# Unread products while the last modulation tile loads, a longer slack for later modulation loads, and a last unit in two halves

## The reference

```python
def adaln(c, w_ada, b_ada):
    mod = jax.nn.silu(c) @ w_ada + b_ada  # (B, 6D)
    return [m[:, None, :] for m in jnp.split(mod, 6, axis=-1)]

sh1, sc1, g1, sh2, sc2, g2 = adaln(c, w_ada[l], b_ada[l])
h = modulate(y_s, norm1_w[l], sh1, sc1)       # rms_norm(x, w) * (1 + scale) + shift
q, k, v, u, g = project_mixers(h, w_in[l], q_norm_w[l], k_norm_w[l])
...
y_s = y_s + g1 * (jnp.concatenate([att, sgu], axis=-1) @ w_o[l])
h = modulate(y_s, norm2_w[l], sh2, sc2)
y_s = y_s + g2 * sq_relu_mlp(h, w_ff1[l], w_ff2[l])
```

## Time and profile before

| | |
|---|---|
| Time, median of 3 runs | 2461.25 us (2461.22 to 2461.75) |
| The profiled execution | 2461.3 us |
| Span of its slowest core (core 7) | 2459.1 us |
| Spans of the other cores | 2451.1 to 2458.5 us |
| TensorE busy, core 7 | 2356.5 us (96%) |
| VectorE, ScalarE, GpSimd busy, core 7 | 1066.5, 721.3, 207.4 us |
| Mean granted clock of TensorE | 0.980 to 0.982 |

### The profile page before, as it was taken

One profiled execution on the slowest core, in us unless ns is written; L12 is line 12 of the kernel. 1 busy time (PEld: TensorE's weight loads), 2 busy tenths in 40 slices (PEclk: granted clock), 3 DMA queues, 4 the chain that ended last, 5 costly groups with the idle time before them and its releaser, 6 DMA issues.

```text
span 2459.1 us, 38418 instructions; the slowest of 8 cores (2451.1 to 2459.1 us)
## 1 busy us (share of the span) xinstructions
PE 2356.5 (96%) x16224; PEld 1351.2 (55%) x16224; DVE 1066.5 (43%) x2129; ACT 721.3 (29%) x1185; POOL 207.4 (8%) x376
## 2 busy tenths in 40 slices
PE   2578999999999999999999999999999999999999
PEld 2367888787888854444444444444444444444444
DVE  2148763754732153553101332322524626528347
ACT  3056675765746561322231001001010010010110
POOL 2101121121100030000110000000000000000000
PEclk7679999999999999999999999999999999999999
DMA  9995786886625186966562222222433423323346
GB/s 208 171 218 156 110 118 94 110 115 111 101 50 83 32 135 140 255 202 129 87 108 52 52 52 52 52 52 52 90 65 64 90 52 75 80 50 81 64 94 188
DMA packets 168728, 251.56 MB, mean 102 GB/s; under 512 B 101104, under 2 KB 106864, under 8 KB 154480
## 3 DMA queue, kind: packets, MB, share of 16 engines
q0 software_dynamic: 54240, 164.94, 39.0%
q1 hardware_dynamic: 114320, 84.17, 13.9%
HBM read 348.28 MB, written 32.67 MB: 155 GB/s over the span
## 4 chain that ended last, share of the span: by engine, by line
PE 92%; DMA 5%; ACT 1%; another core or an unknown queue 1%; DVE 0%; POOL 0%; issue 0%; DVEq 0%; POOLq 0%
PE ps L454 92%; DMA ada<-wa 3%; DMA wr<-wa 1%; DMA xt<-xs 1%; ACT xn L487 0%; PE ps L464 0%; ACT hT L487 0%; POOL ada L575 0%; ACT P L487 0%; DVE xn L516 0%; DVE hT L516 0%; POOL wr L575 0%; ACT mod L487 0%; ACT st L497 0%
## 5 line engine op out<-in xcount | busy, mean ns | idle before, releaser
L454 PE MATMUL ps<-wf,aT 128*128 128x512 bf16 x3072 | 665.0, 379 | 0.0
L454 PE MATMUL ps<-hT,wf 128*128 128x512 bf16 x3072 | 665.0, 379 | 0.0
L454 PEld LDWEIGHTS ps<-hT,wf 128*128 128x128 bf16 x3072 | 300.4, 98 | 362.2 <-issue 0.8
L454 PEld LDWEIGHTS ps<-wf,aT 128*128 128x128 bf16 x3072 | 300.1, 98 | 362.5 <-issue 0.8
L487 ACT ACTIVATE tm<-ps 128x512 f32<-128x512 f32 x192 | 114.3, 597 | 1029.4 <-PE ps L454 1029.4
L454 PE MATMUL ps<-wr,hT 128*128 128x256 bf16 x3072 | 373.7, 277 | 6.9 <-DVE hT L516 4.6
L509 DVE TENSOR_TENSOR aT<-tm 128x512 bf16<-128x512 f32 x192 | 132.7, 692 | 548.8 <-ACT tm L487 546.0
L487 ACT ACTIVATE P<-ps 128x1024 bf16<-128x1024 f32 x304 | 295.8, 1020 | 128.9 <-PE ps L454 128.6
L454 PEld LDWEIGHTS ps<-wr,hT 128*128 128x128 bf16 x3072 | 297.3, 100 | 55.1 <-issue 18.5
L509 DVE TENSOR_TENSOR acc<-acc,ps 128x512 f32<-128x512 f32 x216 | 148.4, 687 | 157.5 <-PE ps L454 156.5
L454 PE MATMUL ps<-VV,P 128*128 128x129 bf16 x2432 | 164.1, 220 | 0.1
(11 more groups left out here) (144 smaller groups left out, 1460.7 us busy)
## 6 DMA issues: line engine op xcount, KB each, us to landing
wf<-wf POOLq DMA_DIRECT2D x64, 1024.0 KB, 8.5
wr<-wa POOLq DMA_DIRECT2D x96, 256.0 KB, 7.5
ada<-wa POOLq DMA_DIRECT2D x32, 512.0 KB, 44.0
xt<-xs POOLq DMA_DIRECT2D x14, 1024.0 KB, 8.2
wr<-wqkv POOLq DMA_DIRECT2D x48, 256.0 KB, 11.6
x1d<-xw SPq DMA_DIRECT2D x12, 1024.0 KB, 5.3
x1b<-x1d SPq DMA_DIRECT2D x48, 256.0 KB, 3.7
wo<-wo POOLq DMA_DIRECT2D x32, 256.0 KB, 15.7
```

Source lines behind the costliest of these rows:

```text
L454: ins = e.matmul(o, lhsT=l, rhs=r, start=st, stop=sp, skip_group_check=True)
```

## The change

A new thread `warm` starts when the first quarter of the last of the eight modulation tiles (tile 7) has come in the plan, and runs until `h_ev[3]` has fired. Whenever TensorE is idle and has nothing queued in the plan, and a PSUM bank is free, it posts two products of the identity with 256 columns of `scT`, at the lowest priority and without a latency at the end, and gives the bank back; nothing reads the result. ADA_SLACK goes from 2000 to 4000 ns for all 32 later modulation tiles. The unit of the last round, the last column block and the last token tile is computed, gated, added and stored in two halves of 256 columns; all other units stay whole.

```diff
--- before.py
+++ after.py
@@ -29,7 +29,7 @@
 
 PE_SWITCH = 100.0
 DMA_RATE = 315.0
-ADA_SLACK = 2000.0
+ADA_SLACK = 4000.0
 ROW_SLACK = 6000.0
 STORE_SLACK = 6000.0
 DMA_LAT = 1900.0
@@ -448,7 +448,7 @@
     def is_ps(self, ap):
         return self.tens[ap.tensor.name][0] == "p"
 
-    def mm(self, ops, mode="full", cost=None, prio=None):
+    def mm(self, ops, mode="full", cost=None, prio=None, lat=LAT["pe"]):
         def fn(e):
             for o, l, r, st, sp in ops:
                 ins = e.matmul(o, lhsT=l, rhs=r, start=st, stop=sp, skip_group_check=True)
@@ -456,7 +456,7 @@
         if cost is None:
             cost = sum(count(o[2]) / 2.4 + 2.5 for o in ops) * 1.01
         return self.post("pe", cost, lambda: self.add("pe", fn, reads=[x for o in ops for x in (o[1], o[2])],
-                                                      writes=[o[0] for o in ops]), LAT["pe"], mode=mode, prio=prio)
+                                                      writes=[o[0] for o in ops]), lat, mode=mode, prio=prio)
 
     def tr(self, ops, ident):
         def fn(e):
@@ -860,6 +860,17 @@
             banks.give(j)
             if u % 2 == 1:
                 mod_ev[u // 2].fire()
+
+    def warm():
+
+        yield ada_ev[7][0]
+        while not h_ev[3].done:
+            if S.busy["pe"] or S.q["pe"] or not banks.free:
+                yield 40.0
+                continue
+            j = banks.free.pop()
+            yield S.mm([(bank(j)[:, 0:256], identb, scT[:, 0:8, :], True, True)] * 2, prio=99, lat=0.0)
+            banks.give(j)
 
     def norm_x(tt):
         yield xev[tt]
@@ -1579,9 +1590,9 @@
             yield S.tt(aT[:, fc, tb * 512:(tb + 1) * 512], rl, rl, ALU.mult)
             tms.give(rl)
 
-        def out2(j, rd, nb, tt, op):
+        def out2(j, rd, nb, tt, op, c0=0, n=512):
             r = 0 if tt < 4 else 1
-            c = slice(nb * 512, (nb + 1) * 512)
+            c = slice(nb * 512 + c0, nb * 512 + c0 + n)
             fold = FOLD + tt % 4
             yield op
             if rd == 0:
@@ -1599,9 +1610,9 @@
                     x1t.give(0)
             else:
                 tf = yield tms
-                yield S.tt(tf, bank(j), g2_t[:, r, c], ALU.mult)
+                yield S.tt(tf[:, 0:n], bank(j)[:, 0:n], g2_t[:, r, c], ALU.mult)
                 banks.give(j)
-                yield S.tt(acc[:, tt, c], acc[:, tt, c], tf, ALU.add)
+                yield S.tt(acc[:, tt, c], acc[:, tt, c], tf[:, 0:n], ALU.add)
                 tms.give(tf)
                 if rd == 7:
                     S.store(yrows(tt)[:, c], acc[:, tt, c], "acc%d" % tt)
@@ -1631,9 +1642,10 @@
                 for tt in range(12):
                     if nb == 0 and tt % 4 == 0:
                         yield [a_ev[fc, tt // 4] for fc in range(8)]
-                    b = yield banks
-                    op = S.mm([(bank(b), aT[:, fc, tt * 128:(tt + 1) * 128], W[:, fc, :], fc == 0, fc == 7) for fc in range(8)])
-                    S.spawn(out2(b, rd, nb, tt, op), 20)
+                    for c0, n in ((0, 512),) if (rd, nb, tt) != (7, 3, 11) else ((0, 256), (256, 256)):
+                        b = yield banks
+                        op = S.mm([(bank(b)[:, 0:n], aT[:, fc, tt * 128:(tt + 1) * 128], W[:, fc, c0:c0 + n], fc == 0, fc == 7) for fc in range(8)])
+                        S.spawn(out2(b, rd, nb, tt, op, c0, n), 20)
                 op.then(lambda k=k: wfs.give(wfbuf[k]))
 
     nc.scalar.preload_act_table_set(LN_SET)
@@ -1650,6 +1662,7 @@
     S.spawn(early_mod(), 5)
     for t0, n in ((6, 2), (8, 4), (12, 4), (16, 4)):
         S.spawn(late_group(t0, n), 12)
+    S.spawn(warm(), 50)
     S.spawn(proj0(), 14)
     S.spawn(w_loads(), 4)
     S.spawn(ada1(), 16)
```

## The result

The change made the kernel **slower**: 2474.6 us (median) against 2461.65 for the kernel before beside it, ratio 1.0052 with a 95% interval of 1.0038 to 1.0065, some 13 us. Some executions of any kernel show one die at a lower granted clock and take far longer (here one of six, 2636.45 us with 0.91 to 0.92); the ratios leave them out, and for the run with the slack alone that leaves two executions of five. The forecast was 2462.3 us, in a range of 2457.3 to 2465.5; the time lies outside the range, and above rival D.

A forecast was written before the change was run, and what follows sets the result against it. TensorE, busy 96% of the span, was taken as the bound. Core 0: 2458.5 + 1.75 (products) - 1.3 (slack) + 1.2 (halves) = 2460.15, the slowest span 1.05 us longer; time 2462.3 us, range 2457.3 to 2465.5.

The forecast's parts named there:

- rival D: Attention stage: slack removes no wait, or a moved load makes TensorE wait once more; 2463.6 to 2464.9 us; chance 0.13.
- 14.6 + 1.9: Tile 7, core 0: 14.6 us from first quarter to projections at full pace, plus 1.9 us lost on half-pace products.
- A: Tile 7: clock falls as the unread products start, and they outlast the gaps; 2462.3 us; chance 0.43.
- C: Tile 7: unread products don't raise the clock and run at 0.50 in all gaps; 2476.6 us; chance 0.07.
- 0.5 to 1.75: Start of the projections: loss from the unread products, about 0.5 us on core 7, 1.75 us on core 0.
- B: Tile 7: clock stays up through the unread products, projections at full pace at once; 2460.5 us; chance 0.27.
- The train: Late modulation tiles, each load issued after the previous tile's products: up to 48 us longer, last products by 709, not 661.
- rival E: Clock stays up and all other waits between 260 and 620 us go, 3.8 us on core 7; 2457.3 us; chance 0.10.
- the 1.9 us of the waits listed: Attention stage, core 7: two TensorE waits for late modulation tiles, 1.9 us together, which the longer slack would remove.

## Why the prediction was wrong, point by point

**The unread products: right.** Exactly 57 pairs. On core 0 the projections start at 151.66 us:

```profile
135.42 4.90 PE L454 MATMUL ps<-scT,identb 128*128 128x256 bf16 x28
...
146.79 0.40 PE L454 MATMUL ps<-ada,scT 128*32 128x512 bf16 x4
147.12 1.27 PE L454 MATMUL ps<-scT,identb 128*128 128x256 bf16 x10
148.23 0.95 PE L454 MATMUL ps<-sel_t,mod 128*128 128x2 f32 x8
149.04 2.78 PE L454 MATMUL ps<-scT,identb 128*128 128x256 bf16 x24
151.66 0.60 PE L454 MATMUL ps<-wr,hT 128*128 128x256 bf16 x4
```

From the first product that is 16.24 us; the forecast was 14.6 + 1.9 = 16.5. The clock fell on all eight cores as the products started and was back about 3 us later, as in A, and C is refuted: the time near C's comes from the slack. The price was sized a little high: from the column sums of tile 6 to the first transposes the median core went from 30.8 to 31.4 us, 0.55 us in place of 0.5 to 1.75. In other runs of 114 products the clock stayed up on up to six of eight cores, as in B (29.5 us for the same way), so A and B are both real and share the cores. What decides between them on a core stays open.

**The halves: right.** 1.2 us forecast, 1.05 measured, and by the mechanism named, the second store held by its key; the run with two keys shows it.

**The slack: wrong, and this decided.** Four steps failed.
- "No new wait from this shows in the trace; I bound it ... to +1.3 us (one more on the slowest core)." I took the bound of a new wait from the waits that were there, all of one kind: TensorE for a late tile. The new wait is of another kind, at another place, and took 13.2 us of standstill, and 4.5 us more were lost at half pace.
- I named the loads that move with each tile, but looked only at what queues behind them on POOL. I didn't ask which transfers of other queues would then be in flight. In the trace of before the question could be put: on core 5 late tiles at 515.33 and 529.23 us on POOL, two transposes from 520.50 to 528.66 on SP, scores from 531.07 on. Moving a load of 2 MB by some microseconds was enough. Beside the loads issued from 529.23 on, the trace of before even shows a slow transpose, issued at 538.16, for which nothing waited:

```profile
DMA to landing us min/median/max: 16.1/16.1/16.1
```

- I priced the wait without the clock. On core 5 each standstill of 6 to 7 us was followed by 3 to 6 us at half pace.
- The train was to end by 709 us; on core 5 its last product is at 747.3. Without the two loads' bytes it is at 728.7 there: some 19 us come from the collisions, the other 20 from the new order, which counting the slack (24 x 2 us) leaves out. The train now runs past the second hand-over, where before no late tile was left.

Rival D had the sign and the cause ("a moved load makes TensorE wait once more"), but one wait of 1.3 us, a tenth of what came. That "the new order of the attention stage makes TensorE wait several microseconds" was named as a way to be wrong, and in the chances it was no more than a tail of D.

**A gain that I under-sized.** Without the collisions the slack saves 4.3 us in the attention stage (585.95 on core 7 before, 581.66 on the same core without the two loads' bytes), not the 1.9 us of the waits listed, and more than rival E's 3.8 us for that core. Of it 2.6 us are idle time of TensorE (3.87 us before, 1.24 here); the other 1.65 are busy time between the two cuts (582.08 and 580.43 us), which hold a few products more in before, so not all of it need be a gain. With all bytes and a slack of 3000 it is 3.5 us.

**Given back.** That a delay at the start "is taken up in the wait for the late x tiles" was named as a way to be wrong; in the run with 76 products a gain was taken up there.

## What to carry to other kernels

When an edit shifts DMA transfers in time, list every other transfer that someone waits for at once, on all queues, and ask which of them will now share the DMA engines with the shifted bytes; the price of such a collision is the landing time under load minus the cover ahead of the reader, plus half of the stretch at half clock behind the standstill. In a kernel whose order comes from a planner, one constant is not one edit: compare the new order at each hand-over with the old one, and to measure a part alone, tell the planner the old cost. A wait that has always been covered does not show in a list of waits, so bounds taken from that list are bounds only for the old order.

## What the runs showed of the hardware

- From 515 to 540 us on core 5, the transposes on SP's queue landed in a median of 9.7 us, 13.2 at worst, beside a load of 2 MB from POOL's queue, and in 4.7 us with most of that load's bytes taken out. Beside the load, from 536 to 537 us, the DMA engines were busy 0.92 of the time at only 131 GB/s.
- Products with an identity as stationary operand, issued as matmuls, bring TensorE's clock back up: in the changed kernel it fell to 0.50 as they began and was at 1.00 again about 3 us later, on all eight cores, while they ran. With 57 products of 32 columns it stayed at 0.50 until the projections had run for 3 to 5 us.
- On the chip of the runs with 76 and with tiny products (the first time each) the granted clock went from 1.00 to 0.81 on all eight cores from 155 to 159 us on, in dense projections, for 8 to 15 us, and the kernel before took 2475.9 us (median) there. The Trainium skill, page "TensorE: Matmul & The Clock Gate", section "Part 1: The HAM clock gate (the "warmup" mystery)", tells of a limiter to 13/16 of the clock once three cores of a die run dense matmuls, held while the load lasts. The level, 0.81, agrees; the rest does not: the clock was back at 1.00 with dense projections still running (core 0 with 76 products, from 170.2 us on), and with 76 products on another chip it showed 1.00 from 155 to 179 us on all eight cores.
